# Decode group of a two-path decoder step: weights of the last head, row loads and the choice of heads re-placed

## The reference, cut to what matters

```
kg = kv_all[:, idx]                            # wp + t - dil * arange(m+1): 129 rows of each branch
sc = einsum('ntgre,ntjge->ntgrj', qh, kg[:, :, :, 0]) * HEAD_DIM ** -0.5
lse = logsumexp(sc);  p = exp(sc - lse)
o = einsum('ntgrj,ntjge->ntgre', p, kg[:, :, :, 1])
...
wts = softmax(stack(lses, axis=0), axis=0)
o = einsum('gnth,gnthe->nthe', wts, stack(outs, axis=0))
x = x + o.reshape(n, t, 1024) @ w_o            # then the MLP
```

## Time and profile before

| | |
|---|---|
| time, median of 3 runs | 2862.43 us (2861.31 to 2862.93) |
| time of the profiled execution | 2860.89 us |
| its span, first to last instruction | 2859.1 us |
| PE busy | 2698.0 us, 94% of the span |
| DVE, ACT, POOL busy | 1367.1, 833.4, 269.3 us |
| mean granted TensorE clock | 0.968 |
| span of the decode group on PE | 1878.10 to 1988.11 us |

### The profile page before, as it was taken

One profiled execution on the slowest core, in us unless ns is written; L12 is line 12 of the kernel. 1 busy time (PEld: TensorE's weight loads), 2 busy tenths in 40 slices (PEclk: granted clock), 3 DMA queues, 4 the chain that ended last, 5 costly groups with the idle time before them and its releaser, 6 DMA issues. The chain is left out here.

```text
span 2859.1 us, 44529 instructions
## 1 busy us (share of the span) xinstructions
PE 2698.0 (94%) x18682; PEld 2564.0 (90%) x18682; DVE 1367.1 (48%) x2273; ACT 833.4 (29%) x1682; POOL 269.3 (9%) x435
## 2 busy tenths in 40 slices
PE   5589999999999999999999999887999999999998
PEld 4478999999999999988888888655999999999998
DVE  7972135423333334756666766655264333333325
ACT  7221122111111112345454454543041111111112
POOL 2300000000000000012232434310000000000000
PEclk7689999999999999999999999988999999999999
DMA  3411111111111111323335546556111111111101
GB/s 96 79 37 50 53 40 49 36 50 49 44 44 44 44 44 45 100 69 79 80 87 134 125 105 144 186 196 228 45 45 45 45 44 44 44 44 44 44 30 61
DMA packets 174495, 205.28 MB, mean 72 GB/s; under 512 B 47334, under 2 KB 129686, under 8 KB 174088
## 3 DMA queue, kind: packets, MB, share of 16 engines
q1 hardware_dynamic: 154512, 159.29, 18.5%
q0 software_dynamic: 19840, 44.00, 6.0%
HBM read 156.73 MB, written 27.82 MB: 65 GB/s over the span
## 5 line engine op out<-in xcount | busy, mean ns | idle before, releaser
L217 PE MATMUL PS<-XH,WH 128*128 128x352 f32 x1920 | 617.8, 322 | 3.7 <-PEq L103 3.7
L218 PE MATMUL PS<-XL,WH 128*128 128x352 f32 x1920 | 619.0, 323 | 0.0
L396 PE MATMUL PS<-HIDH,WH 128*128 128x352 f32 x1536 | 494.9, 323 | 8.1 <-DVE HIDL L331 8.1
L397 PE MATMUL PS<-HIDL,WH 128*128 128x352 f32 x1536 | 494.5, 323 | 0.0
L221 PE MATMUL PS<-XH,WL 128*128 128x352 f32 x1920 | 414.9, 324 | 0.0
L217 PEld LDWEIGHTS PS<-XH,WH 128*128 128x128 f32 x1920 | 362.4, 189 | 4.2 <-issue 4.1
L218 PEld LDWEIGHTS PS<-XL,WH 128*128 128x128 f32 x1920 | 361.3, 188 | 0.1
L347 DVE TENSOR_TENSOR H<-PS,H 128x1056 f32<-128x1056 f32 x128 | 160.8, 1256 | 391.5 <-PE PS L400 391.1
L400 PE MATMUL PS<-HIDH,WL 128*128 128x352 f32 x1536 | 331.6, 324 | 0.0
L221 PEld LDWEIGHTS PS<-XH,WL 128*128 128x128 f32 x1920 | 329.4, 188 | 0.0
L396 PEld LDWEIGHTS PS<-HIDH,WH 128*128 128x128 f32 x1536 | 289.3, 188 | 12.7 <-DVE HIDL L331 12.7
(11 more groups left out here) (384 smaller groups left out, 3427.0 us busy)
## 6 DMA issues: line engine op xcount, KB each, us to landing
RAW<-w_up SPq DMA_DIRECT2D x32, 1024.0 KB, 5.3
RAW<-w_down SPq DMA_DIRECT2D x32, 1024.0 KB, 4.9
KVR<-cache_kv_w SPq DMA_DIRECT2D x18, 1024.0 KB, 10.1
QB<-QA SPq DMA_DIRECT2D x120, 132.0 KB, 2.5
ARAW<-w_q SPq DMA_DIRECT2D x24, 512.0 KB, 4.7
O_SCRATCH<-OT POOLq DMA_DIRECT2D x96, 128.0 KB, 2.7
OB<-O_SCRATCH POOLq DMA_DIRECT2D x24, 512.0 KB, 6.4
RAW<-w_glu SPq DMA_DIRECT2D x16, 512.0 KB, 4.7
```

The source lines that it names most:

```text
L217: nc.tensor.matmul(out, wh(k), xh[:, k, c], start=(k == 0), stop=False)
L218: nc.tensor.matmul(out, wh(k), xl[:, k, c], start=False, stop=False)
L396: nc.tensor.matmul(out, w, m.hidh[:, k, q], start=(k == 0), stop=False)
L397: nc.tensor.matmul(out, w, m.hidl[:, k, q], start=False, stop=False)
```

## The change

- Rows of head 2: their six loads move from the head of the decode group into the attention phase, behind step 89's output store on POOL (u = 90), with the three waits for the key and value outputs.
- Maxima of head 3: POOL stores them ahead of the last output store. SP loads them back ahead of three cache loads (1 MB each) instead of behind.
- Weights of head 3: maxima combined in step 0, weights in step 1, turned in step 2. POOL stores them and loads the rows behind piece 5, instead of behind piece 7.
- ACT waits for the output stores just before its first copy to `SPT`.
- `choose` is two transposes of `OSB` (128 columns each) and takes both value heads of a half; `place` picks the right columns with four copies of 64x2x4x2 instead of two of 64x8x4. `PICK` and its five set-up instructions go.
- Piece 11 moves from step 6 to step 7, behind the last mask.
- At the end ACT splits `w_o`'s first block before step 7's copies to `SPT`, and the decode columns after two blocks instead of six; DVE places step 7's heads before `low(0)`.

```diff
-PIECES = {0: (0, 1), 1: (2, 3), 2: (4, 5), 4: (6, 7), 5: (8, 9), 6: (10, 11)}
+PIECES = {0: (0, 1), 1: (2, 3), 2: (4, 5), 4: (6, 7), 5: (8, 9), 6: (10,), 7: (11,)}
...
@@ attention_phase, gpsimd
         for u in range(N_STEPS + 1):
+            if u == N_STEPS:
+                mix.pool_maxima(pool, 3)
...
-        for i in range(RO):
-            pool.wait_ge(o_st[i], 16 * o_stores(N_STEPS, i))
-        pool.wait_ge(k_st, 16 * k_stores(N_GR))
-        pool.wait_ge(v_st, 16 * k_stores(N_GR))
-        pool.wait_ge(new_st, 32 * N_GR)
+            if u == 90:
+                pool.wait_ge(k_st, 16 * k_stores(N_GR))
+                pool.wait_ge(v_st, 16 * k_stores(N_GR))
+                pool.wait_ge(new_st, 32 * N_GR)
+                mix.pool_rows(pool, 2, mix.made, 3)
@@ sample_phase, sync
         sp.wait_ge(s.pv, N_STEPS)
+        mix.load_maxima(sp, 3, mix.ml_late)
         for u, j in ((4, 1), (4, 5), (5, 2)):
             load(u, j)
-        mix.load_maxima(sp, 3, mix.ml_late)
@@ sample_phase, gpsimd
-        mix.pool_rows(pool, 2, mix.made, 3)
-        mix.pool_maxima(pool, 3)
-        for p in range(2, 8):
+        for p in range(2, 6):
             mix.pool_piece(pool, p)
         mix.pool_weights(pool, 3)
+        for sem, n in s.o_stored:
+            pool.wait_ge(sem, n)
         mix.pool_rows(pool, 3, mix.rows, 1)
-        for p in range(8, 12):
+        for p in range(6, 12):
             mix.pool_piece(pool, p)
@@ sample_phase, scalar
-        for sem, n in s.o_stored:
-            act.wait_ge(sem, n)
...
+            if u == 7:
+                act.wait_ge(scores, 8)
+                wo.hi(act, 0)
             act.wait_ge(p_turned, u + 1)
...
+            if u == 0:
+                for sem, n in s.o_stored:
+                    act.wait_ge(sem, n)
...
+            if u == 1:
+                mix.act_exp(act, 3)
             if u == 2:
-                mix.act_exp(act, 3)
-            if u == 3:
                 act.wait_ge(mix.turned, 4)
                 mix.act_keep(act, 3, ps[0:96, 6, 384:512])
-            if u == 7:
-                act.wait_ge(scores, 8)
-                wo.hi(act, 0)
...
-            if k == 5:
+            if k == 1:
                 act.wait_ge(placed, 8)
@@ sample_phase, vector
-        nc.vector.memset(s.pick[:], 0.0).then_inc(pick_zero, 1)
...
-            src = ps[0:64, 6, 256:384].rearrange("p (n k r) -> p k n r", n=4, r=2)
-            for r in range(2):
-                dst = s.at_s[64 * r:64 * r + 64].rearrange("p k (n t) -> p k n t", t=TS)
-                ins = nc.vector.tensor_copy(dst[:, :, 4 * g:4 * g + 4, t], src[:, 0:KT, :, r])
+            for e in range(2):
+                src = ps[64 * e:64 * e + 64, 6:8, :].rearrange("p b c -> p (b c)")[:, 256:528].rearrange("p (j c) -> p j c", j=2)
+                src = src[:, :, 0:128].rearrange("p j (n h r) -> p r j n h", n=4, r=2)[:, :, :, :, 2 * e:2 * e + 2]
+                for r in range(2):
+                    dst = s.at_s[64 * r:64 * r + 64].rearrange("p (j e k) (n t) -> p e t j n k", j=2, e=2, t=TS)
+                    ins = nc.vector.tensor_copy(dst[:, e, t, :, 4 * g:4 * g + 4, :], src[:, r])
...
+            if u == 0:
+                mix.dve_maxima(dve, 3)
             if u == 1:
-                mix.dve_maxima(dve, 3)
-            if u == 2:
                 mix.dve_weights(dve, 3)
         wo.lo(dve, 0)
+        keep_o(7)
+        place(7)
         low(0)
-        keep_o(7)
-        low(1)
-        place(7)
-        for k in range(2, 4):
-            low(k)
...
-        for k in range(4, KT):
+        for k in range(1, KT):
             low(k)
@@ sample_phase, tensor
-            for kv in range(NKV):
-                mm = nc.tensor.matmul(ps[0:64, 6, 256:384], s.osb[:, u % 2, 64 * kv:64 * kv + 64], s.pick[:, kv, :],
-                                      start=(kv == 0), stop=(kv == NKV - 1))
+            for j in range(2):
+                mm = nc.tensor.transpose(ps[:, 6, 256 + 128 * j:384 + 128 * j], s.osb[:, u % 2, 128 * j:128 * j + 128], m.ident[:])
...
-            if u == 3:
+            if u == 2:
                 mix.pe_turn(pe, 3, ps[0:96, 6, 384:512]).then_inc(mix.turned, 1)
```

More of the change, by code:

```diff
@@ L1379, in __init__ @@
         self.smask = at("SMASK", [128, 2, 480], F32, HIDH_AT + 18432)
-        self.pick = at("PICK", [128, NKV, 128], F32, HIDH_AT + 22656)
         self.qbl = at("QBL", [128, 3, 2, NSMP, 32], F32, RAW_AT + 16384)
@@ L2268, in sample_phase @@
     scores, masked, neg, expd, rec, normed = (sig(n) for n in ("scores", "masked", "neg", "expd", "rec", "normed"))
-    p_turned, kept_p, pv, kept_o, picked, placed, pick_set = (sig(n) for n in (
-        "p_turned", "kept_p", "pv", "kept_o", "picked", "placed", "pick_set"))
-    pick_zero, x_in, s_hi, x_hi, x_lo, s_lo = (sig(n) for n in ("pick_zero", "x_in", "s_hi", "x_hi", "x_lo", "s_lo"))
+    p_turned, kept_p, pv, kept_o, picked, placed = (sig(n) for n in ("p_turned", "kept_p", "pv", "kept_o", "picked", "placed"))
+    x_in, s_hi, x_hi, x_lo, s_lo = (sig(n) for n in ("x_in", "s_hi", "x_hi", "x_lo", "s_lo"))
     s.s_lo = s_lo
@@ L2398, in _ @@
         dve.wait_ge(s.pv, N_STEPS)
-        nc.vector.memset(s.pick[:], 0.0).then_inc(pick_zero, 1)
-        dve.wait_ge(pick_zero, 1)
-        for kv in range(NKV):
-            ins = nc.vector.tensor_copy(s.pick[:, kv, :].rearrange("p (n h) -> p n h", n=4)[:, :, 4 * kv:4 * kv + 4],
-                                        m.ident[:].rearrange("p (n h) -> p n h", n=4)[:, :, 4 * kv:4 * kv + 4])
-        ins.then_inc(pick_set, 1)
         def keep_o(u):
@@ L2502, in choose @@
             pe.wait_ge(kept_o, u + 1)
-            if u == 0:
-                pe.wait_ge(pick_set, 1)
-            for kv in range(NKV):
-                mm = nc.tensor.matmul(ps[0:64, 6, 256:384], s.osb[:, u % 2, 64 * kv:64 * kv + 64], s.pick[:, kv, :],
-                                      start=(kv == 0), stop=(kv == NKV - 1))
+            for j in range(2):
+                mm = nc.tensor.transpose(ps[:, 6, 256 + 128 * j:384 + 128 * j], s.osb[:, u % 2, 128 * j:128 * j + 128], m.ident[:])
             mm.then_inc(picked, 1)
```

## The result

| | before | after |
|---|---|---|
| median of five runs | 2862.43 us | 2846.53 us |
| lowest and highest | 2861.31 to 2862.93 | 2838.79 to 2847.78 |
| profiled execution, its span | 2860.89, 2859.1 | 2846.91, 2845.1 |
| decode group, first score to the product's first matmul | 110.01 | 96.54 |

The ratio is 0.9947, 95% interval 0.9936 to 0.9957: 15.9 us faster in the median, where 20.0 were forecast. The runs of the changed kernel lie up to 9 us apart, those of the kernel before 1.6 us here, but 8 to 10 on the chips of the experiments.

The account below looks back on a forecast made before the run. PE was taken to bound decode steps at 10.30 us, with losses from waits and low clock. Savings of 3.2 + 4.6 + 0.2 + 6.7 + 2.9 + 2.4 = 20.0 us took 2862.4 to 2842.4 us; range 2838 to 2853 (8 in 10).

Parts of the forecast that it names:

- rival 2: Clock still falls once or twice, at the start or in step 4, 5.6 us each: 2848 to 2853.6 us; chance 13%.
- Start, −3.2: Group's first window: ACT no longer waits before the key copies, PE's 3.30 us gap becomes 0.40; 3.2 us saved.
- Step 0, −4.6: Decode step 0: clock stays at 1.00, small loads arrive in time, maxima added; 11.35 us against 15.96.
- Steps 1 to 3, −0.2: Decode steps 1 to 3: 10.9, 11.8 and 9.9 us as weights move to step 1; net about 0.2 us saved.
- Choose: choose in each step: two transposes for 1.09 us of PE work, worth nearly nothing alone because the key copy follows.
- Step 4, −6.7: Decode step 4: head 3's rows arrive 5 us early, so wait and low clock go; 10.6 us against 17.33.
- Step 6, −2.9: Decode step 6: with piece 11 gone, keep_o(6) starts 2.9 us sooner, which the following chain gains.
- step 7, −2.4: From step 7's probability transposes to the product's first matmul: 9.6 us against 12.00.
- Slower: Rival: PE activity too thin in most steps, clock low at 5.6 us a step, up to 2876 us; chance 3%.
- does not do what it says: Rival: another wait, such as a cache load for keys, behind each removed one; 2855 to 2864 us; chance 4%.
- third rival: Same as Slower: PE too thinly busy without choose's matmuls, 5.6 us for each low-clock step; chance 3%.

Follow-up runs that it names:

- second set: The changed kernel run once more, unchanged, on another call's chip, with a second profile: 2842.35 us, ratio 0.9949 to the kernel before.
- start undone: Changed kernel with all output stores awaited at the head of the phase and head 2's rows loaded there: 2845.74 us, ratio 0.9958.
- old choose and third load later: Changed kernel with choose and place as before, and the third cache load behind step 1's values: 2841.77 us, ratio 0.9946.
- cache loads first: Changed kernel with SP's three 1 MB cache loads ahead of the sixteen small loads, as before: 2850.82 us, ratio 0.9969.
- third load later: Changed kernel with the third of SP's three cache loads moved behind step 1's values: 2843.17 us, ratio 0.9943.
- start alone: Kernel before, with only ACT's later wait for the output stores and head 2's rows loaded at u = 90: 2852.76 us, ratio 0.9976.
- end alone: Kernel before, with only piece 11 in step 7, ACT's two moves and step 7's heads placed before low(0): 2853.53 us, ratio 0.9981.
- choose alone: Kernel before, with only the new choose and place: 2859.21 us, ratio 1.0003.
- old choose: Changed kernel with choose and place as before (four matmuls against PICK, two copies): 2842.67 us, ratio 0.9943.
- both edits: Changed kernel with choose and place as before and the cache loads ahead of the small loads: 2849.22 us, ratio 0.9962.
- transposes thrice: Two kernels, the changed one with choose's two transposes given three times: without (2845.38 us) and with the third cache load behind step 1's values (2841.01 us).
- choose three times: Changed kernel with choose's two transposes given three times, same data to the same place, cache loads unmoved: 2845.38 us, ratio 0.9954.

## Why the prediction was right, and where it was not

The measured 2846.53 us lies in the range of 2838 to 2853, and just outside the forecast's own range of 2838.5 to 2846. The sign came as said, and 15.9 of 20.0 us. In the profile the group gained 13.5 us of the 20.0; the range holds the result because it allowed for a falling clock (rival 2), which came, but in other steps and at another price. The median of the second set, 2842.35 us, is the forecast to 0.1 us, and that is luck: in its profile the group took 94.92 us, 4.9 more than the forecast's 90.0, and began at 1871.51, 6.6 us sooner than in the kernel before, which no part of the change explains. Point by point:

- *Start, −3.2.* Right: 3.3 (6.20 us). Its reason was half right. In the changed kernel two edits each remove the wait for the store: ACT's later wait, and SP's order, which lets the store land sooner. The run with the start undone, with a first window of 6.33 us, shows the second to be enough; what the start part then brings are the early rows of head 2. On the kernel before, where the cache loads go first, the start part was worth 5.5 of the 8.5 us expected of it.
- *Step 0, −4.6.* Right in the profile of the changed kernel: 11.19 for 11.35 us. The small loads came in time, but the margin was as narrow as the prediction had it. SP's first one went out 1.6 us into the group there, and DVE did not wait; at 3.2 us, with old choose and third load later, DVE waited 0.37 us; at 6.1 us, with cache loads first, 4.37. (In the changed kernel's second profile it was 3.5 us and DVE did not wait, but the low clock in step 0 had made DVE later there.) But the clock is not as safe here as the term said: in four profiles in which nothing made step 0 wait it ran low for part of it (0.86 or 0.87).
- *Steps 1 to 3, −0.2.* **This is the term that failed.** Measured +6.6 us (39.36 against 32.79). By 0.7 us it is piece 3's load, which I had not followed through the queues: issued at 1892.07 behind 3 MB, it landed at 1900.96. The runs with the cache loads first (4.4 us for that load) and with the third load later (10.83 us for the step) show it. By 6.1 us it is the clock. The prediction held these steps at 1.00 because the earlier trace rows have 1.00 there, and gave no price to the case that they would not, except as a rival. The second rival priced a fall at 5.6 us and put it at the start or in step 4; it came in steps 2 and 3, and mostly shorter: about 1.6 us each time, 4.6 once.
- *Choose.* Right that it brings nearly nothing: alone 1.0003. The score matmuls wait for the key copy, as the 0.68 us at 1921.25 show.
- *Step 4, −6.7.* Right: 10.49 us for 10.6, 10.48 to 10.50 in all five profiles that have the new choose as it is on the changed kernel. No run has the weights' part alone. But every kernel without it took 16.54 to 18.78 us in step 4 (the kernel before, start alone, end alone, choose alone), and every one with it 10.48 to 10.86.
- *Step 6, −2.9 and step 7, −2.4.* Right: 9.21 for 9.2, and 9.85 for 9.6; `place` took 0.08 us more than its 0.7, and the other 0.2 us stay open. Alone the end was worth 4.8 for 5.3.
- *Slower, and does not do what it says.* Neither came. No key transpose waited for a cache load.

What makes the clock fall in the steps? Take the windows of steps 1 to 3 in all profiles, without step 1 of the two kernels with cache loads first, which follows 4 us of stall. With the new choose as it is (the changed kernel twice, choose alone, third load later, cache loads first, start undone) 8 of 17 are below 1.00. With the old choose (the kernel before, old choose, start alone, end alone, both edits, old choose with the third load later) it is 1 of 17, and with the transposes thrice 0 of 6. That speaks for the thinner choose. It would be the third rival's mechanism, at a fraction of its size, since a fall came in some steps and cost 1.6 us and not 5.6. But it is a count over few profiles, and which execution was profiled weighs in it: those of choose alone and third load later lie 3 us above their kernel's median, those of start alone and end alone 1 to 2 us below, and those with the transposes thrice are each the fastest of five. (The changed kernel's second profile is the fastest of its five too, and has two of the eight.) It is not shown in time: old choose, thrice and plain differ by less than their intervals, and choose alone has the ratio 1.0003. Nor is it shown in the granted clock of whole executions, whose mean is 0.972 for the changed kernel run again, 0.973 and 0.972 for the two with the old choose and the changed SP order, and 0.971 and 0.973 for the two with the transposes thrice.

Whether transposes hold the clock as matmuls do stays open too. The profiles with six transposes kept 1.00 in steps 1 to 3, as those with four matmuls did. But the other four runs of choose three times had a mean granted clock of 0.969 to 0.971, where the profiled one had 0.974, and they took 7 to 8 us longer. By the rule weighed in the prediction (the Trainium skill, TensorE: Matmul & The Clock Gate, Part 4: PE-mode transpose) transposes are not counted as matmuls are, and thrice should be as thin as once. The times fit that; the windows of the two profiles do not.

Choose cannot be the only cause. Step 0 ran low without a stall ahead of it with the old choose too (start alone). Why one execution falls in a step and the next does not stays open, and with it how much of the spread of 9 us between runs of one kernel (2838.8 to 2847.8) is the clock's: a part of it lies outside the group, which began at 1875.90 and at 1871.51 us in the changed kernel's two profiles.

## What to carry to other kernels

A step's length read at the full clock holds only for executions in which the clock stays up, and a sum of such steps needs a price for those in which it does not: here 1.6 us per short fall, 4.6 for the long one. Whoever takes matmuls out of a chain that waits anyway wins next to nothing there (ratio 1.0003); that it also makes the clock fall is suggested here by a count of windows, not shown. One profile of a kernel whose runs lie 9 us apart is a single sample, and it helps to note where in the spread it lies. Where small loads on a chain and large loads for later share a queue, put the small ones first, but then follow what else is issued behind the large ones: here a 512 KB load landed 1.2 us late. And two edits may remove one wait, so undo each alone before either is given the credit.

## What the runs showed of the hardware

A fall of the clock to 1.2 GHz did not need a gap like the 3.30 us ahead of it before. In the changed kernel it came behind 1.58 us of waiting, 0.44 of work and 0.20 of waiting. In step 3 of five profiles (the changed kernel twice, choose alone, start undone, old choose with the third load later), it came with no wait over 0.9 us in the step ahead of it, around the probability copies.

The store of 96 KB of maxima was seen by the waiting SP after 2.2 us in three profiles (1875.33 to 1877.50 in the changed kernel) and after 3.9 to 4.2 us in five (1870.94 to 1875.04 in the changed kernel again), with no cache load issued in the 5 us before it. With 3 MB of cache loads issued around it, it took 6.6 and 6.8 us. A load of 512 KB took 4.4 and 4.5 us with no cache load just ahead of it, 8.7 to 8.9 us behind 3 MB, and 8.0 to 8.7 us behind 2 MB.
